# Twenty expert rows moved from the third tile's stages to the channel mixer, its gelu two column tiles on, and one weight slab loaded a stage earlier

## The reference

```python
def peer_ffn(h, w_q, sub_keys, expert_u, expert_v):
    q = (xb @ w_q).reshape(PEER_BLOCK, PEER_HEADS, 2, PEER_HALF)
    s = jnp.einsum('thjd,hjkd->thjk', q, sub_keys)
    sv, si = lax.top_k(s, PEER_TOPK)
    cand = sv[:, :, 0, :, None] + sv[:, :, 1, None, :]
    cs, ci = lax.top_k(cand.reshape(...), PEER_TOPK)
    eidx = i1 * PEER_N_KEYS + i2
    g = jax.nn.softmax(cs, axis=-1)
    act = jax.nn.gelu(jnp.einsum('td,thkd->thk', xb, expert_u[eidx]))
    return jnp.einsum('thk,thkd->td', g * act, expert_v[eidx])
```

## Time and profile before

| what | us |
|---|---|
| median of 3 runs | 3019.01 (3010.56 to 3028.56) |
| the profiled execution | 3031.93 |
| its span, from the first to the last instruction | 3030.2 |
| PE busy | 2395.2 (79%), 9768 matmuls |
| DVE busy | 1747.8 (58%) |
| ACT busy | 575.0 (19%) |
| POOL busy | 1214.1 (40%) |
| software queue's (gathers') share of the 16 DMA engines | 46.4% |
| hardware queue's (slabs' and others') share | 24.7% |

### The profile page before, as it was taken

One profiled execution on the slowest core, in us unless ns is written; L12 is line 12 of the kernel. 1 busy time (PEld: TensorE's weight loads), 2 busy tenths in 40 slices (PEclk: granted clock), 3 DMA queues, 4 the chain that ended last, 5 costly groups with the idle time before them and its releaser, 6 DMA issues. The chain is left out here.

```text
span 3030.2 us, 28174 instructions
## 1 busy us (share of the span) xinstructions
PE 2395.2 (79%) x9768; PEld 1672.6 (55%) x9768; DVE 1747.8 (58%) x3622; ACT 575.0 (19%) x1560; POOL 1214.1 (40%) x1058
## 2 busy tenths in 40 slices
PE   6988899889746866998786953774887836999988
PEld 5847788565644545885552732351764312556755
DVE  3315410279998877476777778768786795000510
ACT  4412300112322220000122102321132000112321
POOL 0000000005887657375554766765665672000000
PEclk9998999989978877999898966887968856999999
DMA  3331233338999999799978897988998996342366
GB/s 144 139 135 42 87 139 142 129 141 340 414 364 351 357 336 406 298 418 414 363 266 297 325 411 292 356 329 352 415 367 331 414 410 259 111 161 101 150 234 245
DMA packets 173229, 832.05 MB, mean 275 GB/s; under 512 B 20881, under 2 KB 21137, under 8 KB 156193
## 3 DMA queue, kind: packets, MB, share of 16 engines
q0 software_dynamic: 147456, 536.94, 46.4%
q1 hardware_dynamic: 25632, 293.33, 24.7%
HBM read 828.09 MB, written 2.10 MB: 274 GB/s over the span
## 5 line engine op out<-in xcount | busy, mean ns | idle before, releaser
L1192 POOL DMA_INDIRECT expert_rows<-in_peer_u,chosen x512 | 666.4, 1302 | 1028.6 <-DVE chosen L1768 668.3
L1192 POOL DMA_INDIRECT expert_rows<-in_peer_v,chosen x512 | 544.2, 1063 | 281.1 <-issue 144.4
L1266 DVE SCALAR_TENSOR_TENSOR expert_rows<-expert_rows,u 128x1024 f32<-128x1024 f32 x512 | 602.3, 1221 | 71.4 <-DMA expert_rows<-in_peer_u,chosen 49.1
L2910 PE MATMUL mlp_up<-mlp_xT,mlp_slab 128*128 128x384 f32 (+1 forms) x1024 | 248.2, 399 | 72.9 <-issue 68.0
L1226 PE MATMUL expert_sum<-expert_rows,expert_diag 128*128 128x512 f32 x496 | 244.3, 640 | 32.1 <-ACT expert_diag L1213 23.5
L1276 DVE SCALAR_TENSOR_TENSOR h<-expert_rows,expert_coef,h 128x1024 f32<-128x1024 f32 x194 | 251.5, 1296 | 9.2 <-DMA expert_rows<-in_peer_v,chosen 4.7
L1276 DVE SCALAR_TENSOR_TENSOR u<-expert_rows,expert_coef,u 128x1024 f32<-128x1024 f32 x190 | 246.3, 1296 | 12.6 <-DMA expert_rows<-in_peer_v,chosen 6.1
L2910 PEld LDWEIGHTS mlp_up<-mlp_xT,mlp_slab 128*128 128x128 f32 x1024 | 162.7, 199 | 163.0 <-issue 100.6
L2901 PE MATMUL mlp_down<-mlp_slab,upT 128*128 128x512 f32 x512 | 230.5, 604 | 26.4 <-issue 26.4
L691 PE MATMUL product<-uT,in_slab 128*128 128x272 f32 (+1 forms) x1024 | 237.7, 388 | 8.2 <-DMA in_slab<-in_w_in 8.2
L691 PEld LDWEIGHTS product<-uT,in_slab 128*128 128x128 f32 x1024 | 191.7, 191 | 39.7 <-issue 8.7
(11 more groups left out here) (545 smaller groups left out, 3281.5 us busy)
## 6 DMA issues: line engine op xcount, KB each, us to landing
in_slab<-in_w_in SPq DMA_DIRECT2D x34, 2048.0 KB, 7.6
mix_slab<-in_w_in SPq DMA_DIRECT2D x16, 2048.0 KB, 9.1
mlp_slab<-in_w_up SPq DMA_DIRECT2D x16, 2048.0 KB, 8.3
mlp_slab<-in_w_down SPq DMA_DIRECT2D x16, 2048.0 KB, 7.8
expert_rows<-in_w_in SPq DMA_DIRECT2D x9, 2048.0 KB, 7.6
mix_slab<-in_ssd_w_out SPq DMA_DIRECT2D x8, 2048.0 KB, 8.2
out_slab<-in_w_out SPq DMA_DIRECT2D x6, 2048.0 KB, 8.3
mix_slab<-in_sc_w_out SPq DMA_DIRECT2D x4, 2048.0 KB, 8.7
```

The lines of the kernel that those rows point to most:

```text
L1192: pool.indirect_dma_start(out=self.row(n), out_offset=None, in_=self.tables[0 if dot else 1], in_offset=bass.IndirectOffsetOnAxis(ap=picks ...
L1266: dve.scalar_tensor_tensor(self.row(n), self.row(n), 1.0, u, ALU.mult, ALU.mult, accum_out=dot).then_inc(self.rows_used, 1)
L2910: ins = pe.matmul(bank[n % UPS][:, 0:W], slab[i % R][:, k, j * P:(j + 1) * P], xT[:, k, :], start=k == 0, stop=k == KD - 1)
```

## The change

1. In `PLAN_TWO` the attention of tile 2 takes 8 units instead of 24, its output product 6 instead of 10. The sum ahead of the mixer's main stage falls from 341 to 321; the mixer gets 191 units instead of 171 (63 dots and 128 additions).
2. `GELU_AT` goes from 9 to 11.
3. The first z slab of the second half's projection gets a buffer of its own (`in_slab_early`, 16 KB a partition), held from the first half's routing until the end of the projection, and is loaded in the first half's `norm_turn` ahead of the routing, behind the two first query slabs. The projection then loads only the second slab at its head.

```diff
-PLAN_TWO = (20, 72, 22, 86, 48, 8, 8, 36, 24, 10, 4, 3)
+PLAN_TWO = (20, 72, 22, 86, 48, 8, 8, 36, 8, 6, 4, 3)
...
+        third = ExitStack()
+        early = []
...
-                            conv, carry, buffers, half, bg, (small_in, 16 * SMALL_LOADS), *choice[1:])
+                            conv, carry, buffers, half, bg, (small_in, 16 * SMALL_LOADS), *early, *choice[1:])
                     end_stage()
+                    if half:
+                        third.close()
...
+                early.append((third.enter_context(nc.sbuf_tensor("in_slab_early", [P, KD, SLAB], F32, side="right"))[:],
+                              sem("in_landed_early", keep=True)))
...
-                norm_turn("ffn_", part_h[half], None, xT, 0, row_gain_dram=t["ln_ffn"], keep=u[half], bg=bg, ahead=first)
+                coming = [] if half else [(early[0][0], t["w_in"][in_slab(O_Z)], early[0][1])]
+                norm_turn("ffn_", part_h[half], None, xT, 0, row_gain_dram=t["ln_ffn"], keep=u[half], bg=bg,
+                          ahead=first + coming)
...
-        slab = [sbuf(ctx, f"in_slab{i}", [P, KD, SLAB]) for i in range(2)]
+        slab = ([early[0]] if half else []) + [sbuf(ctx, f"in_slab{i}", [P, KD, SLAB])[:] for i in range(1 if half else 2)]
...
-        landed = [sem(f"in_landed{i}") for i in range(2)]
+        landed = ([early[1]] if half else []) + [sem(f"in_landed{i}") for i in range(1 if half else 2)]
...
-            for s in range(2):
-                sp.dma_start(slab[s][:], parts[0][0](s)).then_inc(landed[s], 16)
+            for s in range(1 if half else 0, 2):
+                sp.dma_start(slab[s], parts[0][0](s)).then_inc(landed[s], 16)
...
-    GELU_AT = 9
+    GELU_AT = 11
```

More of the change, by code:

```diff
@@ L603, in project @@
 def project(frame, slab_loader, ident, uT, z, xs, xs_meta, bt, bt_meta, bf, cf, dt, constants, carry,
-            buffers, half, bg, constants_in, choice_exp=None, choice_made=None):
+            buffers, half, bg, constants_in, early=None, choice_exp=None, choice_made=None):
     nc, t, sem, sbuf, psum, block, enter, leave, leave_sync = frame
@@ L645, in _ @@
                 parts.reverse()
-            for s in range(2):
-                sp.dma_start(slab[s][:], parts[0][0](s)).then_inc(landed[s], 16)
-            slab_loader(sp, [s[:] for s in slab], landed, product, 4, parts)
+            for s in range(1 if half else 0, 2):
+                sp.dma_start(slab[s], parts[0][0](s)).then_inc(landed[s], 16)
+            slab_loader(sp, slab, landed, product, 4, parts)
             leave_sync(sp)
```

## The result

The changed kernel took 3050.07 us (median), the kernel before 3019.01. The ratio is 1.0081, with a 95% interval of 1.0056 to 1.0106: 17 to 32 us slower. The ratio compares the runs in the faster of two states (one run of the changed kernel, 3071 us, is left out) and stands for 24 us, where the two medians lie 31 apart. The forecast was 3022 us, with a range up to 3043. The time lies above the range, and it came nearest to rival 2 (half clock and long hold, 3040).

The account below looks back on a forecast made before the run. It took VectorE and half-clock PE together to bound the third tile's attention, and PE, held beside gathers, the mixer's end. Terms 0 - 9 - 1 + 12.7 = +2.7 us, carried to the median 3019, gave 3022 us, range 2992 to 3043.

Parts of the forecast that it names:

- rival 2: Attention stays bound by PE at clock 0.50 (gain 1), mixer's hold lasts till the ring is full (+22): +21, 3040 us; chance 0.22.
- First slab, 0 us: Second half's projection: PE starts 8.4 us sooner, all hidden under VectorE's choice of experts and 12 dots; bounds 0 to -11.4.
- the hold: Mixer: beside gathers that fill the DMA, PE's matmuls slow to 2.79 us each and complete well after issue.
- Attention, -9 us: Third tile's attention: 16 dots fewer end gathers 20.5 us sooner, PE's matmuls then speed up; gain 9, between 1 and 18.9.
- lower bound of 1: Third tile's attention: PE is full at half clock, its stream stays, only small waits go; gain about 1 us.
- Output product, -1 us: Output product: of four dots removed, two were hidden, two delay PE by at most 1.4 us; bounds 0 to -1.4.
- Dots' end, +25.6: Mixer: 20 more dots at the DMA's pace, 1.28 us each, move the dots' end by 25.6 us.
- The gelu, +23: Mixer: hold lasts to 2394, so the gelu two column tiles on comes at 2405 instead of 2382.
- the upper bound: Mixer: PE held until the ring is full, 13 us after the last dot; gelu at +32, less 10.3: +22.
- PE's lead, 10.3: Mixer: at the gelu PE stands two column tiles (32 matmuls, 10.3 us) further and keeps that lead; net +12.7 us.
- Sum: Whole kernel: 0 - 9 - 1 + 12.7 = +2.7 us on the profiled execution, 3022 us as median; chance 0.42.
- Rival 3, PE never waits: Mixer ends by PE's own count, 20 gathers cost nothing, earlier 10 us gain kept: -10, 3009 us; chance 0.05.

Follow-up runs that it names:

- before_k4: Kernel before, but from unit 869 on (the mixer) at most four gathers open instead of sixteen; ratio 0.9848 to before, on a chip with the hold.
- plan_and_gelu: Kernel before with the 20 units moved and the gelu two column tiles later, without the early slab; ratio 1.0022 to before, on a chip without the hold.
- whole_again: The whole changed kernel measured once more against the kernel before, on a chip with the hold; ratio 1.0076.
- before_k6: Kernel before, but with at most six rows open in the mixer's gathers from unit 869 on; ratio 1.0038 to before, on a chip without the hold.

## Why the prediction was wrong, step by step

- **First slab, 0 us: right**, by its own reasoning (8.4 us sooner for PE, nothing for VectorE), and in two runs alone (1.0011, 0.9991), both on chips without the hold.
- **Attention, -9 us: wrong; -0.9 measured**, its lower bound of 1. The step that failed is "near 2228 instead of 2248 ... the matmuls sped up as the gathers ceased". POOL issued its last gather of the stage before 2226, and nothing sped up. The 0.149 us a matmul came from a row in which two heads run side by side, at clock 0.50 like the rest: both rows of 1.19 us lie ahead of the clock's rise. The other price, 0.182, was from a stage at clock 1.00, and nothing in the forecast said why the clock should rise. In these runs relief of VectorE was worth something only where it rose within the stage, in one of the eight profiled executions with 8 dots there.
- **Output product, -1 us: wrong; +1.9.** The two dots gave nothing, and the half clock reached into it.
- **Dots' end, +25.6: right**; 59.9 to 87.0 is +27.1.
- **The gelu, +23: wrong; +40.4** (75.6 to 116.0), and this is the step that decides. I took the length of the hold from one stretch of another stage (1740 to 1776: "Taken over: the hold lasts to 2394"). It lasted until the ring of rows was full, as I had put for the upper bound. The gelu then came 8 us later than that bound: the bound had 49 of the 72 matmuls that it waits for started by the release (17 in the hold and 32 issued ahead), and the trace has 35.
- **PE's lead, 10.3: too small.** The additions took what was forecast. The last addition came 42.8 us later (277.3 against 234.5) and the mixer lost 23.2, so PE's lead was 19.6 us. In matmuls started: at the gelu PE stood at 233 of the mixer's instead of 197, and at the last addition at 362 instead of 320. So 36 of the 42 matmuls of lead, not 32, came before the additions, and most of the rest from a start of the additions at full pace that lasted 31 us instead of 29.
- **Sum**: +2.7 forecast; by stages -0.9 + 1.9 + 23.2 = +24.2, inside the interval of 17 to 32. Rival 2 had both mechanisms right, and its price, +21, nearly; that is partly luck, since its gelu came 8 us too early and its lead was 9 us too small. The chance of 0.22 was too low, and the evidence for it (PE full at 0.50 for the whole 20 us) was better than what I set against it.
- **Rival 3, PE never waits**: true in the mixer on the chips without the hold up to the experts' end, where the moved units and the gelu cost 0.1 to 0.2%; but not the gain of 10 that I gave it, since the experts then end last.

Open: what the hold is. Gathers are needed for it (before_k4) and are not enough (plan_and_gelu at 415 GB/s, PE at full pace, with a dozen gathers in flight there, counted from issues and landings). On a chip with the hold a full DMA doesn't bring it at once either: in whole_again PE starts 48 matmuls in 20 us beside 416 GB/s (2327 to 2347), some 10 us ahead of the hold. What a chip has that makes it so was not found. The Trainium skill, NOTIFIC — the notification-queue block, section "7.1 Overflow: three behaviours, one of which stalls the engine", says that this block's internal pipeline always pushes back on its producers. No run here shows whether an engine's records were behind the hold. Nor were the change's parts, or before_k6, measured where the hold is.

## What to carry to other kernels

Moving work between stages pays only where the engine that bounds the stage is relieved: with PE full at half clock, taking 16 dots from VectorE gave 0.9 us. When two mechanisms in one direction rest on whole tables and the gain rests on one row, price the gain at its bound. And gathers that cost 0.1 to 0.2% on one chip can cost 0.8% on another, so measure a change of this kind on both. A slower pace for gathers that have slack (169 us here, on a chip with the hold) is worth a trial: four open rows gained 1.5% there, three lost 0.7%, and on the chips without the hold six open rows lost 0.2 to 0.4%.

## What the chips showed that was not expected

The same kernel takes 3003 to 3019 us on some chips and 2806 to 2811 on others, some 200 us less. 126 us of that lie in the mixer alone (471.3 against 345.6), where PE completes a matmul each 2.79 us while gathers fill the DMA on the one kind, and each 0.36 us (110 in 40 us) under the same 410 GB/s on the other. With at most four gathers in flight the kernel loses 10.7%, with six 1.0 to 1.4%, both on chips without the hold.
